# Two transformer-like blocks in one kernel: the second block's feed-forward part of tokens 0 to 255 moved into the expert gather

## What is computed

```python
h = h + mixer_sublayer(...)                 # first block: two attentions, gates
h = h + peer_sublayer(h, ...)               # per token 8 heads x 16 experts of 16384:
                                            #   y += gate * gelu(u[e] . norm(h)) * v[e]
# second block, on all 512 tokens
h = rms_norm(x, norm1_g) * (1 + sc1) + sh1
proj = h @ w_in                             # 3088 columns
... gated linear attention, dilated causal attention ...
x = x + g1 * (mixed @ w_out)
h = rms_norm(x, norm2_g) * (1 + sc2) + sh2
u = causal_depthwise_conv(h @ w_up, conv_w, conv_b)     # w_up 1024 x 5632, 3 taps in time
u_gate, u_val = split(u)
x = x + g2 * ((silu(u_gate) * u_val) @ w_down)          # w_down 2816 x 1024
```

## Time and profile before

| | us |
|---|---|
| median of 3 runs | 2731.71 |
| runs | 2725.87 to 2734.3 |
| the profiled execution, its own time | 2735.58 |
| its span in the trace | 2733.8 |

### The profile page before, as it was taken

How to read it: one execution, slowest core, us unless ns; L and a number is a source line. 1 busy time by engine, 2 the same in 40 slices (tenths; PEclk the granted TensorE clock), 3 DMA queues, 4 the chain that set the end, 5 groups by cost and what they waited for, 6 DMA issues and landing times. The chain is left out here.

```text
span 2733.8 us, 25164 instructions
## 1 busy us (share of the span) xinstructions
PE 2214.5 (81%) x7846; PEld 1352.5 (49%) x7846; DVE 1671.2 (61%) x3405; ACT 1017.9 (37%) x2518; POOL 713.1 (26%) x619
## 2 busy tenths in 40 slices
PE   5999868897888777777868887658776967799988
PEld 5778644476533232322324453223333834588777
DVE  5652456544598898878456776647666533555434
ACT  4213235513244333333334444436433433433322
POOL 1000214001244444443434544435442100100000
PEclk8999869998999999898989999878897959799999
DMA  6773200022299999999999999989997511222122
GB/s 198 227 214 97 66 5 23 19 82 102 115 422 420 421 396 421 404 421 404 418 376 420 421 419 418 406 339 407 421 420 288 144 46 47 94 97 102 61 85 100
DMA packets 142490, 682.67 MB, mean 250 GB/s; under 512 B 19440, under 2 KB 36112, under 8 KB 73888
## 3 DMA queue, kind: packets, MB, share of 16 engines
q0 software_dynamic: 73728, 536.90, 47.6%
q1 hardware_dynamic: 68640, 144.30, 16.2%
HBM read 679.05 MB, written 2.10 MB: 249 GB/s over the span
## 5 line engine op out<-in xcount | busy, mean ns | idle before, releaser
L1791 PE MATMUL peer_Y<-peer_w,peer_diag 128*128 128x512 f32 x1792 | 909.5, 648 | 230.6 <-ACT peer_diag L1777 205.1
L1736 POOL DMA_INDIRECT peer_w<-in_peer_uv,peer_eidx x512 | 603.7, 1179 | 757.0 <-PE peer_Y L1791 477.2
L1745 DVE CUSTOM_DVE_ANT_0 peer_w<-peer_w,peer_xtok 128x1024 f32<-128x1024 f32 x512 | 620.3, 1222 | 208.4 <-DMA peer_w<-in_peer_uv,peer_eidx 204.8
L1791 PEld LDWEIGHTS peer_Y<-peer_w,peer_diag 128*128 128x128 f32 x1792 | 342.9, 204 | 746.1 <-ACT peer_diag L1777 428.4
L1769 ACT ACTIVATE peer_gel<-peer_dots 128x1 f32<-128x1 f32 x512 | 103.8, 203 | 723.6 <-DVE peer_dots L1745 719.3
L1777 ACT ACTIVATE peer_diag<-all_ident,peer_a 128x128 f32<-128x128 f32 x448 | 179.9, 402 | 17.4 <-PE peer_Y L1791 2.9
L1771 ACT ACTIVATE peer_a<-peer_gel,peer_gates 128x1 f32<-128x1 f32 x512 | 150.9, 295 | 16.7
L2278 PE MATMUL ffn_acc<-m2f_hs,ffn_cut 128*128 128x512 f32 x352 | 138.3, 393 | 9.4 <-DVE ffn_cut L2326 9.4
L654 DVE TENSOR_TENSOR p_cut<-m1h_raw,p_cut 128x512 fp32r<-128x512 f32 (+2 forms) x96 | 63.2, 660 | 126.3 <-ACT p_cut L680 126.3
L2279 PE MATMUL ffn_acc<-m2f_hs,ffn_cut 128*128 128x512 f32 x352 | 138.0, 392 | 0.0
L2280 PE MATMUL ffn_acc<-m2f_hs,ffn_cut 128*128 128x512 f32 x352 | 137.9, 392 | 0.0
(11 more groups left out here) (466 smaller groups left out, 3823.1 us busy)
## 6 DMA issues: line engine op xcount, KB each, us to landing
m_gates<-in_w_ada SPq DMA_DIRECT2D x48, 512.0 KB, 4.3
m2f_raw<-in_w_up SPq DMA_DIRECT2D x22, 1024.0 KB, 4.8
m1h_raw<-in_w_in SPq DMA_DIRECT2D x80, 256.0 KB, 3.0
m20h_raw<-in_w_in SPq DMA_DIRECT2D x48, 256.0 KB, 7.1
m22h_raw<-in_w_in SPq DMA_DIRECT2D x48, 256.0 KB, 3.2
m_down_ring<-in_w_down SPq DMA_DIRECT2D x22, 512.0 KB, 3.5
peer_w<-in_peer_uv,peer_eidx POOLq DMA_INDIRECT x512
m_out_ring<-in_w_out SPq DMA_DIRECT2D x16, 512.0 KB, 8.6
```

The lines of the kernel that those rows point to most:

```text
L1736: pool.indirect_dma_start(self.w[:, n % self.RW].rearrange("p c n -> p (c n)"), None, self.uv_dram, bass.IndirectOffsetOnAxis(self.col(sel ...
L1745: dve.tensor_tensor_reduce(u, u, self.xtok[:, n // PICKS, :], 1.0, 0.0, ALU.mult, ALU.add, self.col(self.dots, n)).then_inc(self.dotted, 1)
L1791: ins = pe.matmul(self.Y[:, h, :], self.diag[:, i % self.RD, :], self.w[:, n % self.RW, 1, h * BANK:(h + 1) * BANK], start=(k == 0), stop= ...
```

## The change

`second_ffn` is now called twice, each time for two token tiles: once inside `peer_and_front`, after `second_front` and before `finish_gather`, with the pacer (prefix `f0`), and once at the end for tokens 256 to 511 (prefix `f2`). The counts of hosted steps are redistributed: the front part has 10 + 60 + 36 + 40 + 28 = 174 in place of 246, the feed-forward part 8 + 40 + 24 = 72. The sum stays 246, and `finish_gather` keeps its 10. `ffn_up` works by half chunks (units of 128 columns of `w_up`, 44 of them), unrolled in place of a hardware loop; with a host it has two slots for split weights and three for raw ones, alone four and four. Its products have 258 columns: two kept columns of `hs` (`kept.ends`) stand ahead of the 256 tokens, so the convolution's first outputs are right. `w_up` and `w_down` are therefore read, and split, twice. In the hosted half, `gT` lies in memory of `qT` and `xtok` that is free by then, and the first chunks of `w_down` aren't fetched ahead (`ahead=False`).

```diff
@@ out_project
-            for c in range(R, kchunks):
-                sp.wait_ge(lo_made, c - R + 1)
+            for c in range(R if ahead else 0, kchunks):
+                if c >= R:
+                    sp.wait_ge(lo_made, c - R + 1)
...
@@ peer_and_front
         second_front(nc, consts, resid, mod, d, kept, HALF, xtok[:, 0:2, :], qT[:].rearrange("p h q -> p (h q)"), pacer)
+        wide, narrow = qT[:].rearrange("p h (a q) -> p (h a) q", a=2), xtok[:, 0:2, :].rearrange("p t (a q) -> p (t a) q", q=2 * P)
+        second_ffn(nc, consts, resid, mod, d, kept, HALF, lambda c: wide[:, c, :] if c < 2 * PEER_H else narrow[:, c - 2 * PEER_H, :],
+                   xtok[:, 0:2, :], out, pacer)
         finish_gather(nc, gather, pacer.next)
...
@@ ffn_up
+    UNITS = 2 * NF
+    CUT = 2 if side.BANKS else 4
+    LEFT = 2
...
+            for u in range(UNITS):          # tensor
+                bank = acc[:, u % 4, 0:LEFT + tokens]
+                hi, lo = cut[:, u % CUT, 0], cut[:, u % CUT, 1]
+                pe.wait_ge(lo_made, u + 1)
+                if u >= 4:
+                    pe.wait_ge(conved, u // 2 - 1)
+                for k in range(KD):
+                    pe.matmul(bank, hi[:, k, :], hs[:, 0, k, :], start=(k == 0), stop=False)
+                    pe.matmul(bank, hi[:, k, :], hs[:, 1, k, :], start=False, stop=False)
+                    ins = pe.matmul(bank, lo[:, k, :], hs[:, 0, k, :], start=False, stop=(k == KD - 1))
                 ins.then_inc(done, 1)
+                if u % 4 == 3:
+                    side.tensor(pe, u // 4)
...
+            for u in range(UNITS):          # scalar; tail(j): wait done, 2 x bias, wait conved, silu
+                if u >= RAW:
+                    act.wait_ge(landed[u % RAW], 16 * (u // RAW))
+                if u >= CUT:
+                    act.wait_ge(done, u - CUT + 1)
+                act.activation(cut[:, u % CUT, 0], raw[:, u % RAW], ACT.Copy).then_inc(hi_made, 1)
+                if u % 2 and u >= 3:
+                    tail(u // 2 - 1)
+                if u % 4 == 3:
+                    side.scalar(act, u // 4)
...
+            for u in range(UNITS):          # vector
+                dve.wait_ge(hi_made, u + 1)
+                dve.tensor_tensor(cut[:, u % CUT, 1], raw[:, u % RAW], cut[:, u % CUT, 0].bitcast(F32), ALU.subtract).then_inc(lo_made, 1)
+                if u % 2 and u >= 3:
+                    conv(u // 2 - 1)
+                elif u >= 4:
+                    gate(u // 2 - 2)
+                if u % 4 == 3:
+                    side.vector(dve, u // 4)
...
@@ second_front: hosted steps
-                               keep=space, side=side(14, n))
+                               keep=space, side=side(10, n))
-                    beside = side(85, len(jobs) * KD)
+                    beside = side(60, len(jobs) * KD)
...
@@ second_ffn
+            norm_transpose(nc, name + "n", ..., tokens=group, early=[ring, conv], keep=keep, side=side(8, len(group)), col0=2)
+            ffn_up(nc, name + "u", hs, kept.ends, d["w_up"], conv["cw"], conv["cb"], gT, ring, [out_ring] if out_ring else [], tokens,
+                   side(40, NF // 2))
+        if hosted:
+            out_ring = Early(ph.sb("down_ring", [P, 2, D]), lambda raw: [])
+        out_project(nc, name + "o", gT, d["w_down"], NF, resid, out_ring, gate=kept.rows[:, 1, :], out_dram=out, tiles=group,
+                    side=side(24, 2 * NF - 2), ahead=not hosted)
```

More of the change, by code:

```diff
@@ L690, in out_loads, with out_project @@
     return lambda raw: [(raw[:, r, :], w_dram[r * P:(r + 1) * P, :]) for r in range(2)]
-def out_project(nc, name, actT, w_dram, kchunks, resid, ring, gate=None, out_dram=None, tiles=range(NT), side=ALONE):
+def out_project(nc, name, actT, w_dram, kchunks, resid, ring, gate=None, out_dram=None, tiles=range(NT), side=ALONE, ahead=True):
     R = 2
@@ L1924, in peer_and_front @@
                 top = TopK(top_ph, tables["iota"], eidx, gates, picked)
-                peer_query(nc, xs, xtok, row["gain"], qT, ring, row, top, tables["keys"])
+                peer_query(nc, xs, xtok, row["gain"], qT, ring, row, top, tables["keys"], kept.ends)
             Phase.recycle(nc)
@@ L2240, in ffn_loads, with ffn_up @@
 def ffn_loads(w_dram):
[L2242 to L2249, removed]
-        raw = ring.raw
[L2251 to L2258, removed]
+    return lambda raw: [(raw[:, u], w_dram[u // 2][:, u % 2]) for u in range(raw.shape[1])]
+def ffn_up(nc, name, hs, ends, w_dram, cw, cb, gT, ring, early, tokens, side=ALONE):
+    UNITS = 2 * NF
+    CUT = 2 if side.BANKS else 4
+    LEFT = 2
+    with Phase(nc, name) as ph:
+        raw = ring.raw
+        RAW = raw.shape[1]
+        cut = ph.sb("cut", [P, CUT, 2, KD, P], F32R)
+        x = ph.sb("x", [P, 2, 2, tokens])
+        sl = ph.sb("sl", [P, 2, tokens])
+        acc = ph.ps("acc", [P, 4, BANK])
+        landed = [ph.sem(f"landed{r}") for r in range(RAW)]
+        names = ("early_landed", "hi_made", "lo_made", "done", "biased", "tap1", "conved", "silued", "out", "dve_link")
+        early_landed, hi_made, lo_made, done, biased, tap1, conved, silued, out, dve_link = (ph.sem(n) for n in names)
+        block = ph.straight()
         @block.sync
         def _(sp):
[L2262 to L2268, removed]
+            for u in range(RAW, UNITS):
+                sp.wait_ge(lo_made, u - RAW + 1)
+                sp.dma_start(raw[:, u % RAW], w_dram[u // 2][:, u % 2]).then_inc(landed[u % RAW], 16)
             load_early(sp, early_landed, early)
@@ L2290, in _, with tail @@
         @block.scalar
         def _(act):
[L2292 to L2302, removed]
+            def tail(j):
+                act.wait_ge(done, 2 * j + 2)
+                if j >= 2:
+                    act.wait_ge(out, j - 1)
@@ L2308, in chunk @@
[L2308 to L2320, removed]
+                act.wait_ge(conved, j + 1)
@@ new lines, in gate @@
+            def gate(j):
+                dve.wait_ge(silued, j + 1)
+                dve.tensor_tensor(gT(j), sl[:, j % 2, :], x[:, j % 2, 1, :], ALU.mult).then_inc(out, 1)
+            link(dve.tensor_copy(hs[:, :, :, 0:LEFT], ends[:]))
+            dve.tensor_copy(ends[:], hs[:, :, :, tokens:tokens + LEFT].bitcast(F32))
+            for u in range(UNITS):
[7 more added lines that the diff above has]
+                    side.vector(dve, u // 4)
@@ L2396, in second_front @@
         attention(nc, name + "a", consts, at(qT), at(kept.kT), kept.av, None, dilated, 0, DIL_E ** -0.5, mixT[:, 4:8, :], [out_ring],
[L2397 to L2401 removed]
+                  tiles=group, side=side(40, DIL_H * n // 2 + 1))
+        out_project(nc, name + "o", lambda c: mixT[:, c, :], d["w_out_2"], KD, resid, out_ring, gate=kept.rows[:, 0, :], tiles=group, side=side(28, 2 * KD - 2))
```

112 lines of the change are left out of this document (47 added, 65 removed).

## The result

The changed kernel takes 2792.43 us (median of 4 runs, 2789.25 to 2802.84) beside 2733.01 us for the kernel before (4 runs): ratio 1.0227, 95% interval 1.0192 to 1.0261, 59 us slower. The forecast was 79 us slower, 2811 us. The profiled execution took 2793.31 us, its span 2791.5.

What follows compares the result with a forecast made beforehand. The ACT-DVE chain, about as long as the DMA's time in the projection, was taken to bound hosted work: hosted part + 375, front part - 128, end - 168 gave + 79 us, 2811 us; range for 8 in 10 2710 to 2880.

Steps and rivals of the forecast that it cites:

- the 2.3 that the prediction named as a sign of being wrong: Front part: the prediction is wrong if a hosted step there gives back 2.3 us or more.
- The front part: Five hosted stages with 72 steps fewer: 687 to 559 us, 128 given back, ending near 1955.
- The end: Feed-forward part alone at the end, for two token tiles: 402 to 234 us, 168 saved.
- Hosted normalisation and down-projection: Hosted feed-forward part: normalisation with 8 steps 32 us; down-projection, 22 chunks of 5.06 us with 24 steps, 128 us.
- The hosted up-projection: Hosted feed-forward part: eleven rounds of 18.6 us on the chain, with fill and end 215 us.
- Rival B: Same mechanism, harder: late w_up transfers, low clock, up-projection 250 us, front gives back 100; 2894 us; 0.15 together with C.
- the price of a second step in a unit: Front part's projection: a second gather step in a unit costs 1.15 us, a dot product alone.
- the relief of the DMA: Linear and dilated attention: fewer steps also remove some waits for gathered rows; 24 and 25 us given back in all.
- Rival A: DMA stays the only bound: second weight reading adds 82 us, the end saves 168; 2646 us, faster; chance 0.07.
- Its partial form: Front part gives back 2.3 us a step (166), hosted part takes 340 us; 2738 us; chance 0.16.
- Rival C: VectorE's low-part work bounds the end's up-projection, so the end isn't shortened; at most + 20 us; 0.15 together with B.
- Table loads: Hosted up-projection: 22 silu/gelu loads of 1.28 us fall in ScalarE's idle time, costed at nothing; uncovered 28 us.

Runs made afterwards that it cites:

- e2_noload: Changed kernel whose hosted up-projection reuses its first three half chunks of w_up, the other 41 loads left out; 2763.03 us.
- e7_move: Changed kernel with hosted steps moved: front part 146 for 174, up-projection 64 for 40, down-projection 28 for 24; 2783.39 us, ratio 1.0201 to the kernel before.
- e1_raw4: Changed kernel with four raw weight slots in place of three in the hosted up-projection; 2766.85 us, ratio 1.0136 to the kernel before.
- e9_halfrow: Kernel before, each fetch bringing half a row, products and folds using that half, all instructions of the other engines kept; 2543.93 us.
- e5_front174: Kernel before with 174 hosted steps in the front part in place of 246, the other 72 run alone in finish_gather; 2750.69 us.

## Why the prediction was right, and where its terms were not

The sign held, and with it the account: the second half costs more beside the gather than the front part and the end give back. The mechanism, the chain through the queues in order, held for the hosted feed-forward part (e2_noload, and chunks of the down-projection 5.15 us apart for 5.06). In the front part it held in part: a step gave back 2.25 us, between the 1.8 of the sum and the 2.5 of a bound by the DMA, and just short of the 2.3 that the prediction named as a sign of being wrong; 1.9 of it are left when further steps go (e7_move). The front part ended at 1915, not near 1955, and the DMA share in `f0o` was 0.86, not 0.8. The total was off by 19 us, inside the range, and partly by luck: errors of 34 and 14 us one way and of 27 the other cancelled in part.

**The end** (- 168) was right within 2 us (from the first mean square of the normalisation on, 403 to 234, it is - 170), with up 136 for 134 and down 84 for 85. Products of 258 columns run at the pitch of the earlier trace rows, 0.12 us, and the pitch of a down chunk was near that of the earlier trace rows, 3.4 us for 3.3. The 0.22 us for each product of the old down-projection was misread (115.23 us are 502 products, 0.23 each), but nothing hangs on it.

**Hosted normalisation and down-projection** were right, 31 for 32 and 128 for 128. The chunk of 5.06 us by the chain was the right bound there.

**The hosted up-projection** was 27 us too low. The round was right (212 us in e1_raw4 and e2_noload for 215 forecast); what failed is that the third raw slot was named as an upper bound and costed at nothing, although already showed a landing of 14.6 us against some 6 free. Rival B had this term, at 250. That the fourth slot gives it back (e1_raw4) and that removing the loads gives the same (e2_noload) shows it.

**The front part** was 34 us too low in what it gives back: 47 us for 31 in the projection, 35 for 24 in the linear attention, 32 for 25 in the dilated attention; the normalisation (7 for 6) and the output projection (41 for 42) were right. Two steps failed.

In the projection it was the price of a second step in a unit, 1.15 us, a dot product alone. The sum there leaves out the fold, which the other stages have with a quarter (1.45). The two-step row that the prediction read (4.09) has no fold on VectorE; 9 of the 20 full-width ones in the kernel before have one, such as this:

```profile
1450.52 0.61 ACT L680 ACTIVATE m20p_cut<-m20h_raw 128x512 fp32r<-128x512 f32 x1
...
1452.92 1.28 DVE L1754 SCALAR_TENSOR_TENSOR all_resid<-peer_w,peer_a,all_resid 128x1024 f32<-128x1024 f32 x1
...
1455.38 0.20 ACT L1769 ACTIVATE peer_gel<-peer_dots 128x1 f32<-128x1 f32 x1 [1.38 <-DVE peer_dots L1745]
...
1456.25 0.61 ACT L680 ACTIVATE m20p_cut<-m20h_raw 128x512 fp32r<-128x512 f32 x1
```

This unit takes 5.73 us. In the kernel before, units of full width (without a piece of the head normalisation) take 3.45 us with one step and 5.11 with two (means of 22 and 20), so a second step costs 1.7; in e9_halfrow, with half rows, 3.49 and 4.86, so 1.4 are the chain's. 25 second steps fewer are 42 of the 47 us. The level was off too: 8 of the 56 units have 16 columns only and take some 2.5 us, and the changed stage was put at 212 us and took 196.

In the two attentions it was the relief of the DMA. The prediction credited some 4 and 8 us of waits for rows; e9_halfrow leaves up to 12 and 17 to the DMA. With these in place of 4 and 8 the sum gives 32 and 34, for 35 and 32 measured. In the output projection the right number was luck: the prediction had the chain as the longer side (81 us, the DMA's 78), but the share of 1.01 at 84 us says the DMA, and the 98 us of e9_halfrow less 17 steps at 1.45 would put the chain at some 73 (an estimate). The waits themselves were a fair measure of the DMA's part: the earlier trace rows lists 18.2 and 24.0 us for the dilated attention and the output projection, where e9_halfrow saves 17 and 27.

**Rival A** (the DMA the only bound) is refuted by the DMA share of 0.72 and 0.86 in the hosted up- and down-projection, and by the sign. Its partial form had the front part's slope right (2.3 a step, measured 2.25), and failed on the hosted part (340, measured 401). **Rival C** is refuted: `f2u` takes 136 us for 134, with TensorE busy for 132.33 of them.

**Table loads** were rightly costed at nothing: 24 fewer save 3 us. The trace shows no drain behind a load (in 43 of its 71 loads the engine's next instruction starts 1.31 us after the end of the one before, load included); the Trainium skill's 2.66 us a switch (ScalarE: Activation LUTs, What ACT_TABLE_LOAD costs) isn't seen in it.

## What to carry to other kernels

Ask of moved work what the same work costs at its old place, at its new place, and after being split: here the half took 234 us alone where both halves took 402, and that loss was there before any overlap. Host work beside a stream only where both the stream's bound and the in-order chain leave room; here moving 28 steps from one host to another bought 9 to 16 us, and moving 28 more nothing. A ring that covers a landing alone may not cover it beside a full DMA: measure the landing in the neighbour's company and count the slots for that.

## What the runs showed that was not expected

The landing of 512 KB beside the gather, 8.9 us for 4.5 alone, cost 26 us of the whole with three slots and nothing with four. So whether hosting pays turned on one slot: with three the hosted version is no faster than the unhosted split, with four it is 17 us faster, and still behind the kernel before.

At the margin the hosting of the front part was worth little: its last 72 steps cost 2.2 us each there and 2.4 alone (e5_front174), and taking them out made the kernel only 21 us longer (2750.69 for 2729.39, one execution). So a hosted stage can have a DMA share of 0.95 and more, as these have, and still gain little from the overlap.
